# Two weight splits of the next expert ahead of the second half of SwiGLU

## The chip, the cores and the metric

One Trainium2 chip, one core. The time is device microseconds of one execution. The kernel before takes 1336.07 us, the median of three runs.

## The reference

One step of a one-layer streaming encoder over 576 tokens (512 of a prompt, 64 of a running stream): a projection, a pooling mixer beside gated linear attention, a layer norm, and then a mixture of 32 experts of which each token takes four. The change lies in the experts:

```python
def block_fn(args):
    e, rows = args
    xb = x2[rows]
    gu = jnp.dot(xb, w_gu[e]) + b_gu[e]
    gate, up = gu[:, :EXPERT_FF], gu[:, EXPERT_FF:]
    gate = jnp.minimum(gate, SWIGLU_LIMIT)
    up = jnp.clip(up, -SWIGLU_LIMIT, SWIGLU_LIMIT)
    hmid = gate * jax.nn.sigmoid(SWIGLU_ALPHA * gate) * (up + 1.0)
    return jnp.dot(hmid, w_down[e]) + b_down[e]
```

Everything is fp32. `w_gu` is 1024 x 2048 and `w_down` 1024 x 1024 for each expert, 12 MB an expert and 403 MB in all.

## The kernel before

Four engines and the queue of the sync engine run programs of their own and meet at semaphores. The first 290 us or so hold everything up to the router. Then a loop over 32 experts `n` runs on each engine, unrolled in Python. An expert's tokens, up to 96, are gathered from memory by GpSimd (`gather`), transposed by TensorE (`rows`), multiplied and scattered back (`scatter`).

**Weights.** The sync engine loads each expert in six pieces of 2 MB (`load`, line 448) into a ring of eight slots, `ring`. Pieces 0 to 3 are `w_gu`, 4 and 5 are `w_down`. Each load waits until its slot is free: for piece 1 of expert e that is the end of the `down` of expert e-2 (`down_read`), for the others a count of finished low splits (`split_done`).

**Splits.** Matmuls in fp16 need the weights as a high and a low fp16 half. Each piece is two pairs; an expert has ten pairs `p` that are split (the last piece is used in fp32 as it is). For each, ScalarE writes the high half (`hi`, line 802, called through `next_hi(n, p)`) and VectorE the low half (`lo`, line 1618, `next_lo(n, p)`), into four rotating buffers. So `hi` waits for the piece to have landed and for TensorE to have used the pair four before (`unit_used`), and `lo` waits for `hi`.

**One expert on TensorE.** Sixteen `unit`s (line 1173), two to a pair: the first half of gate (pairs 0 and 1, into `bank[2]`), the first half of up (2 and 3, `bank[3]`), then the second half of gate (4 and 5) and of up (6 and 7), both into `wide[0]`. Then the transposes of the next expert's rows, and `down` (line 1194) into `wide[1]`: first the fp16 part with pairs 8 and 9, then a part of 16 fp32 matmuls which reads `hm[:, 4:8]` and `w_down` from the ring, and which waits here:

```python
if k % 4 == 0:
    pe.wait_ge(hm_done, n * 2 + (k // 4 + 3))
```

**One expert on ScalarE.** `hi` of pairs 4 and 5, `gate(n, 0)`, pairs 6 and 7, `up(n, 0)`, pair 8, `hidden_hi`, pair 9, `gate(n, 1)`, `up(n, 1)`, then for the next expert pair 0, `rows_hi`, and pairs 1 to 3, then `weigh`, the output's evacuation. `gate` (line 816) is four evacuations (line 812) and a sigmoid (line 821), `up` (line 823) four evacuations and a clip (line 828).

**One expert on VectorE.** The low splits in the same order; `gated_half` (line 1593) multiplies gate and sigmoid, and `hidden` (line 1595, its instruction on line 1602) multiplies in up and signals `hm_done`. Behind `hidden(n, 1)` stand the low split of pair 0 of the next expert, `rows_lo`, `places_of`, and pairs 1 to 3.

Each engine carries out its program in the written order, so the order of these calls is the schedule. After the experts, the rows of four partial results (`part_rows`) are loaded back and summed with the last two experts' outputs, which TensorE adds, and a layer norm ends the kernel.

Of the kernel before, what the change touches and what calls it, by code (L numbers as in the profile page):

```python
# [50 lines left out]
E = 32  # L51
# [20 lines left out]
def build(nc, x_prompt, x_sample, state_pool, state_gla, w_in, w_pool, pool_scale, w_gate_up,  # L72
# [3 lines left out]
    with ExitStack() as ctx:  # L76
# [304 lines left out]
        def piece_slot(n, i):  # L381
            return (n * PER + i) % RING
# [6 lines left out]
        def landed(n, i):  # L389

            return 16 * (EARLIER[piece_slot(n, i)] + (n * PER + i) // RING + 1)
# [9 lines left out]
        def pair_done(n, p):  # L401

            return pairs(n) + (p + 1 + BUFS)
# [4 lines left out]
        def down_done(n):  # L408

            return n + 3  # L410
# [241 lines left out]
        def _(act):  # L652
# [45 lines left out]
            for t in range(TILES):  # L698
                n = ROWS[t]
# [84 lines left out]
            for t in range(TILES):  # L784
                n = ROWS[t]
# [5 lines left out]
                n = ROWS[t]  # L791
# [3 lines left out]
            def rows_hi(m, q):  # L795

                for b in range(2):
                    act.wait_ge(gT_ready, m * 2 + (b + 1))
                    act.activation(xhi[q][:, 4 * b:4 * b + 4, :], bank[b][:, 0:4 * BLK]
                                   .rearrange("p (k s) -> p k s", k=4), ACT.Copy, scale=X_UP).then_inc(gT_hi, 1)  # L800

            def hi(n, p, s, got):

                if p % 2 == 0:
                    act.wait_ge(slot_in[s], got)
                act.wait_ge(unit_used, pair_done(n, p) - BUFS)
                act.activation(whi[buf(n, p)], packed(s, p), ACT.Copy, scale=W_UP).then_inc(hi_done, 1)  # L807

            def from_limit(dst, b, at):

                for c in range(4):
                    last = act.activation(dst[:, c, :], b[:, c * BLK:(c + 1) * BLK], ACT.Relu, scale=-DOWN * S_UP,  # L812
                                          bias=bguT[:, at[0], at[1] + c:at[1] + c + 1])
                return last

            def gate(n, half, e):
                act.wait_ge(unit_used, pair_done(n, 4 * half + 1))
                act.wait_ge(hm_done, n * 2 + (half + 2))
                from_limit(g1, bank[2] if half == 0 else wide[0][:, 0:512], (e, 4 * half)).then_inc(gate_free, 1)
                act.wait_ge(gate_free, n * 2 + (half + 3))  # L820
                act.activation(sg, g1, ACT.Sigmoid, scale=-SWISH / S_UP, bias=sig_bias).then_inc(sig_done, 1)  # L821

            def up(n, half, e):
                act.wait_ge(unit_used, pair_done(n, 4 * half + 3))
                act.wait_ge(hm_done, n * 2 + (half + 2))
                from_limit(u1, bank[3] if half == 0 else wide[0][:, 512:1024], (e, 8 + 4 * half)).then_inc(up_free, 1)
                act.wait_ge(up_free, n * 2 + (half + 3))
                act.activation(u1, u1, ACT.Relu, scale=-1.0, bias=up_bias).then_inc(up_clip, 1)  # L828

            def hidden_hi(n):  # L830
                act.wait_ge(hm_done, n * 2 + 3)
                act.wait_ge(unit_used, pair_done(n - 1, 9))
                act.activation(hh, hm[:, 0:4, :], ACT.Copy, scale=1.0 / S_UP).then_inc(hh_done, 1)

            def weigh(n, p):

                act.wait_ge(down_read, down_done(n))
                if not isinstance(n, int):
                    act.wait_ge(scattered, n * 16 - 32)
                elif n > 0:  # L840
                    act.wait_ge(scattered, n * 16)
                act.activation(orow, wide[1 if isinstance(n, int) else 0][0:BLK, :], ACT.Copy, scale=slots[p][:, 5:6])\  # L842
                   .then_inc(out_ready, 1)

            def next_hi(n, p):
                hi(n, p, piece_slot(n, p // 2), landed(n, p // 2))
# [5 lines left out]
            for n in range(E):  # L852
                next_hi(n, 4)
                next_hi(n, 5)
                gate(n, 0, n)
                next_hi(n, 6)
                next_hi(n, 7)
                up(n, 0, n)
                next_hi(n, 8)
                hidden_hi(n)  # L860
                next_hi(n, 9)
                gate(n, 1, n)
                up(n, 1, n)
                if n + 1 < E:
                    next_hi(n + 1, 0)
                    rows_hi(n + 1, (n + 1) % 2)
                    next_hi(n + 1, 1)
                    next_hi(n + 1, 2)
                    next_hi(n + 1, 3)
                if n == 4:  # L870
                    act.wait_ge(bd_in, 16)
                    act.activation(y30_hi[BLK:P, :], bd, ACT.Copy)
                    act.activation(y31_hi[BLK:P, :], bd, ACT.Copy).then_inc(bd_hi, 1)
                if n + 2 < E:
                    weigh(n, n % ROW_BUFS)
                elif n + 1 < E:
                    act.wait_ge(down_read, down_done(n))
                    act.activation(y30_hi[0:BLK, :], wide[1][0:BLK, :], ACT.Copy, scale=slots[n % ROW_BUFS][:, 5:6])\
                       .then_inc(y30_high, 1)
# [27 lines left out]
            for t in range(RUN):  # L907
                n = HOLD
# [399 lines left out]
        def _(dve):  # L1308
# [6 lines left out]
            for t in range(TILES):  # L1315
                n = ROWS[t]
# [179 lines left out]
            for t in range(TILES):  # L1496
                n = ROWS[t]
# [92 lines left out]
            def gated_half(n, half):  # L1590

                dve.wait_ge(sig_done, n * 2 + (half + 1))
                dve.scalar_tensor_tensor(g1, g1, -LIMIT * S_UP, sg, ALU.add, ALU.mult).then_inc(gated, 1)  # L1593

            def hidden(n, half):

                dve.wait_ge(gated, n * 2 + (half + 1))
                dve.wait_ge(up_clip, n * 2 + (half + 1))
                dve.wait_ge(down_read, n + 2)
                if half == 0 and isinstance(n, int) and n > 0:  # L1600
                    dve.wait_ge(hh_done, n)
                dve.scalar_tensor_tensor(hm[:, 4 * half:4 * half + 4, :], u1, (1.0 - LIMIT) * S_UP, g1, ALU.add, ALU.mult)\  # L1602
                   .then_inc(hm_done, 1)

            def hidden_lo(n):
                dve.wait_ge(hh_done, n + 1)
                dve.scalar_tensor_tensor(hl, hm[:, 0:4, :], 1.0 / S_UP, hh, ALU.mult, ALU.subtract).then_inc(hl_done, 1)  # L1607
# [10 lines left out]
            def lo(n, p, s):  # L1618

                dve.wait_ge(hi_done, pairs(n) + (p + 1))  # L1620
                dve.wait_ge(unit_used, pair_done(n, p) - BUFS)
                dve.scalar_tensor_tensor(wlo[buf(n, p)], packed(s, p), W_UP, whi[buf(n, p)],  # L1622
                                         ALU.mult, ALU.subtract).then_inc(split_done, 1)

            def next_lo(n, p):
                lo(n, p, piece_slot(n, p // 2))
# [16 lines left out]
            for n in range(E):  # L1643
                if n + 2 < E:
                    onehot(n + 2, n + 2)
                next_lo(n, 4)
                if n == E - 1:
                    dve.wait_ge(y30_high, 1)
                    dve.scalar_tensor_tensor(y30_lo[0:BLK, :], wide[1][0:BLK, :], slots[(E - 2) % ROW_BUFS][:, 5:6],
                                             y30_hi[0:BLK, :], ALU.mult, ALU.subtract).then_inc(out_ready, 1)  # L1650
                next_lo(n, 5)
                gated_half(n, 0)
                next_lo(n, 6)
                next_lo(n, 7)
                hidden(n, 0)
                if n + 2 < E:
                    rows_of(n + 2, (n + 2) % ROW_BUFS, n - 2 if n >= 2 else None)
                if n == 1:
                    counts()
                if n == 5:  # L1660
                    dve.wait_ge(bd_hi, 1)
                    dve.tensor_tensor(y30_lo[BLK:P, :], bd, y30_hi[BLK:P, :], ALU.subtract).then_inc(bd_split, 1)
                if n == 6:
                    dve.memset(gatesT, 0.0).then_inc(gatesT_zero, 1)
                next_lo(n, 8)
                hidden_lo(n)
                next_lo(n, 9)
                gated_half(n, 1)
                hidden(n, 1)
                if n + 1 < E:  # L1670
                    next_lo(n + 1, 0)
                    rows_lo(n + 1, (n + 1) % 2)
                    places_of(n + 1, (n + 1) % ROW_BUFS)
                    next_lo(n + 1, 1)
                    next_lo(n + 1, 2)
                    next_lo(n + 1, 3)
            dve.wait_ge(unit_used, pair_done(E - 1, 9))
# [118 lines left out]
```

## Time and profile before

| | |
|---|---|
| time, median of three runs (lowest, highest) | 1336.07 us (1336.06, 1338.35) |
| the profiled execution: its time, its span | 1336.07 us, 1334.3 us |
| TensorE busy | 1254.9 us, 94% |
| VectorE busy | 1042.6 us, 78% |
| ScalarE busy | 941.8 us, 71% |
| GpSimd busy | 167.6 us, 13% |
| mean DMA rate | 354 GB/s |
| mean granted clock of TensorE | 0.983 |

The shares are means over the whole span, with the 290 us before the experts and the last 40 us in them. In a row of the order in time, the first number is the start in us from the span's start, the second how long the row's instructions take together; then the engine, the line, the operation, what it writes and reads, how many instructions are merged (x), and in square brackets the idle time ahead and what ended it. PE is TensorE, ACT ScalarE, DVE VectorE, SPq the queue of the sync engine.

### The profile page before, as it was taken

The page shows a single profiled execution, that of the slowest core. Times are in us where ns is not written, and L with a number is a line of the kernel's source. Part 1 is how long each engine was busy: PE and PEld are TensorE (multiplying, and loading weights), DVE is VectorE, ACT ScalarE, POOL GpSimd, SP SyncE. Part 2 cuts the span into 40 slices and gives each one's busy share as a digit, 9 for nine tenths or more (in the row PEclk, how much of TensorE's full clock was granted, in tenths as well). Part 3 has the DMA queues.
Part 4 walks back from the last instruction along what each step waited for, and adds up shares of the span by engine and source line. Part 5 has one row for each costly group of instructions (what it writes and reads, how often), then busy time and mean ns, then how long its engine had stood idle before and what let it go on. Part 6 is the DMA issues. An engine that isn't in the chain of part 4 may idle for free.

```text
span 1334.3 us, 35273 instructions
## 1 busy us (share of the span) xinstructions
PE 1254.9 (94%) x15514; PEld 902.6 (68%) x15514; DVE 1042.6 (78%) x1205; ACT 941.8 (71%) x1230; POOL 167.6 (13%) x139
## 2 busy tenths in 40 slices
PE   6999989979999999999999999999999999999985
PEld 3446655457777777777777777777777777777742
DVE  4442345478888899989989888888888888888877
ACT  4541221038888988899889888888888888888931
POOL 1000821011100001110010000111101111111002
PEclk9999999979999999999999999999999999999988
DMA  9550046059999999999999999999999999999983
GB/s 319 206 212 1 7 180 273 31 210 404 414 410 424 425 425 426 424 425 425 425 425 426 424 426 425 425 426 424 425 425 424 426 425 422 425 424 424 413 373 96
DMA packets 51033, 472.66 MB, mean 354 GB/s; under 512 B 9566, under 2 KB 10357, under 8 KB 25661
## 3 DMA queue, kind: packets, MB, share of 16 engines
q1 hardware_dynamic: 38860, 436.22, 78.3%
q0 software_dynamic: 11360, 31.77, 6.3%
q8 instruction: 125, 2.05, 0.6%
q10 hardware_dynamic: 656, 2.36, 0.5%
q14 instruction: 32, 0.25, 0.0%
HBM read 450.63 MB, written 29.95 MB: 360 GB/s over the span
## 4 chain that ended last, share of the span: by engine, by line
PE 38%; DMA 26%; DVE 6%; ACT 5%; issue 4%; SPq 0%; DVEq 0%; ACTq 0%; POOLq 0%
PE wide L917 27%; DMA ring<-in_w_gu 18%; PE bank L917 10%; DMA ring<-in_w_down 5%; ACT work L807 3%; DVE work L1622 3%; DMA work<-part_rows 2%; ACT work L812 1%; PE bank L1166 1%; DVE ring L1749 0%; DVE ring L1747 0%; DMA work<-h_rows,work 0%; DVE ring L1736 0%; DVE work L1607 0%; ACT work L828 0%
## 5 line engine op out<-in xcount | busy, mean ns | idle before, releaser
L1622 DVE SCALAR_TENSOR_TENSOR work<-ring,work 128x2048 f16<-128x2048 f32 x320 | 721.4, 2287 | 109.7 <-ACT work L807 95.3
L807 ACT ACTIVATE work<-ring 128x2048 f16<-128x2048 f32 x320 | 599.4, 1902 | 90.5 <-DMA ring<-in_w_gu 65.1
L917 PE MATMUL wide<-work 128*128 128x96 f16 (+3 forms) x7048 | 485.7, 230 | 36.9 <-DVE work L1607 10.9
L917 PEld LDWEIGHTS wide<-work 128*128 128x128 f16 (+3 forms) x7048 | 374.9, 102 | 131.9 <-issue 46.7
L917 PE MATMUL wide<-ring,work 128*96 128x512 f32 (+4 forms) x888 | 345.8, 545 | 1.0 <-ACT work L744 1.0
L917 PEld LDWEIGHTS bank<-work 128*128 128x128 f16 (+2 forms) x6482 | 296.8, 100 | 36.0 <-issue 23.7
L917 PE MATMUL bank<-work 128*128 128x96 f16 (+3 forms) x6482 | 304.6, 208 | 8.3 <-ACT work L780 3.8
L917 PEld LDWEIGHTS wide<-ring,work 128*96 128x96 f32 (+4 forms) x888 | 133.5, 151 | 190.0 <-issue 161.1
L607 POOL DMA_INDIRECT work<-h_rows,work x32 | 62.0, 1939 | 466.6 <-PE bank L1166 445.0
L620 POOL DMA_INDIRECT part_rows<-work x30 | 43.6, 1454 | 379.6 <-ACT work L842 379.6
L812 ACT ACTIVATE work<-wide,work 128x96 f32<-128x96 f32 x256 | 64.9, 333 | 0.1
L812 ACT ACTIVATE work<-bank,work 128x96 f32<-128x96 f32 x256 | 64.8, 333 | 0.0
L842 ACT ACTIVATE work<-wide,work 96x1024 f32<-96x1024 f32 x30 | 33.1, 1102 | 35.0 <-PE wide L917 35.0
L821 ACT ACTIVATE work<-work 128x384 f32<-128x384 f32 x64 | 39.4, 616 | 2.1
L828 ACT ACTIVATE work<-work 128x384 f32<-128x384 f32 x64 | 39.4, 616 | 2.1
L1500 DVE SCALAR_TENSOR_TENSOR ring<-ring,wide 128x1024 f32<-128x1024 f32 (+1 forms) x5 | 6.1, 1220 | 43.0 <-PE wide L917 43.0
L780 ACT ACTIVATE work<-bank 128x512 f32<-128x512 f32 (+1 forms) x10 | 5.0, 552 | 49.0 <-PE bank L1094 49.0
L917 PE MATMUL wide<-work,ring 128*128 128x512 f16 (+2 forms) x296 | 37.6, 285 | 0.0
L1602 DVE SCALAR_TENSOR_TENSOR work<-work 128x384 f32<-128x384 f32 x64 | 35.6, 556 | 1.4 <-DVE work L1593 0.2
L1166 PE MATMUL bank<-work 128*128 128x128 f32 x256 | 34.3, 277 | 2.0 <-DMA work<-h_rows,work 1.9
L1593 DVE SCALAR_TENSOR_TENSOR work<-work 128x384 f32<-128x384 f32 x64 | 35.3, 552 | 0.0
L1329 DVE SCALAR_TENSOR_TENSOR ring<-ring 128x1024 f16<-128x1024 f32 x16 | 19.0, 1222 | 20.9 <-ACT ring L695 20.9
(197 smaller groups left out, 637.8 us busy)
## 6 DMA issues: line engine op xcount, KB each, us to landing
ring<-in_w_gu SPq DMA_DIRECT2D x128, 2048.0 KB, 28.9
ring<-in_w_down SPq DMA_DIRECT2D x64, 2048.0 KB, 33.6
part_rows<-work POOLq DMA_DIRECT2D x1, 10240.0 KB, 36.8
ring<-in_w_in SPq DMA_DIRECT2D x4, 2048.0 KB, 13.6
ring<-part_rows SPq DMA_DIRECT2D x3, 2560.0 KB, 27.5
ring<-in_w_out SPq DMA_DIRECT2D x2, 2048.0 KB, 9.3
h_rows<-work POOLq DMA_DIRECT2D x1, 2560.0 KB, 9.9
ring<-h_rows SPq DMA_DIRECT2D x1, 2560.0 KB, 24.8
```

Of the source, the lines that this page charges most:

```text
L607: pool.indirect_dma_start(xg, None, h_dram, bass.IndirectOffsetOnAxis(ap=tok_i[q], axis=0), bounds_check=PLACES - 1, oob_is_err=False)\
L620: pool.indirect_dma_start(part_dram, bass.IndirectOffsetOnAxis(ap=dst_i[p], axis=0), orow, None, bounds_check=TOPK * SPAN - 1, oob_is_err= ...
L807: act.activation(whi[buf(n, p)], packed(s, p), ACT.Copy, scale=W_UP).then_inc(hi_done, 1)
L812: last = act.activation(dst[:, c, :], b[:, c * BLK:(c + 1) * BLK], ACT.Relu, scale=-DOWN * S_UP, bias=bguT[:, at[0], at[1] + c:at[1] + c + 1])
L821: act.activation(sg, g1, ACT.Sigmoid, scale=-SWISH / S_UP, bias=sig_bias).then_inc(sig_done, 1)
L828: act.activation(u1, u1, ACT.Relu, scale=-1.0, bias=up_bias).then_inc(up_clip, 1)
L842: act.activation(orow, wide[1 if isinstance(n, int) else 0][0:BLK, :], ACT.Copy, scale=slots[p][:, 5:6])\
L917: return pe.matmul(out, w, x, start=start, stop=stop, skip_group_check=True)
L1166: last = pe.transpose(bank[b][:, k * BLK:k * BLK + P], xg[:, (4 * b + k) * P:(4 * b + k + 1) * P], used)
L1593: dve.scalar_tensor_tensor(g1, g1, -LIMIT * S_UP, sg, ALU.add, ALU.mult).then_inc(gated, 1)
L1602: dve.scalar_tensor_tensor(hm[:, 4 * half:4 * half + 4, :], u1, (1.0 - LIMIT) * S_UP, g1, ALU.add, ALU.mult)\
L1622: dve.scalar_tensor_tensor(wlo[buf(n, p)], packed(s, p), W_UP, whi[buf(n, p)], ALU.mult, ALU.subtract).then_inc(split_done, 1)
```

## The change

Both programs call the same functions as before. On ScalarE the high splits of pairs 0 and 1 of the next expert move from behind `up(n, 1)` to between `gate(n, 1)` and `up(n, 1)`. On VectorE the low splits of the same pairs move to between `gated_half(n, 1)` and `hidden(n, 1)`. Pair 1 also moves ahead of `rows_hi`, and of `rows_lo` and `places_of`. The last expert has no next one and keeps its order.

```diff
                 hidden_hi(n)
                 next_hi(n, 9)
                 gate(n, 1, n)
+                if n + 1 < E:
+                    next_hi(n + 1, 0)
+                    next_hi(n + 1, 1)
                 up(n, 1, n)
                 if n + 1 < E:
-                    next_hi(n + 1, 0)
                     rows_hi(n + 1, (n + 1) % 2)
-                    next_hi(n + 1, 1)
                     next_hi(n + 1, 2)
                     next_hi(n + 1, 3)
                 if n == 4:
@@
                 hidden_lo(n)
                 next_lo(n, 9)
                 gated_half(n, 1)
+                if n + 1 < E:
+                    next_lo(n + 1, 0)
+                    next_lo(n + 1, 1)
                 hidden(n, 1)
                 if n + 1 < E:
-                    next_lo(n + 1, 0)
                     rows_lo(n + 1, (n + 1) % 2)
                     places_of(n + 1, (n + 1) % ROW_BUFS)
-                    next_lo(n + 1, 1)
                     next_lo(n + 1, 2)
                     next_lo(n + 1, 3)
```

## Rows read from the trace of the kernel before

**Rows 1.** The page: DMA rate in 40 slices; a line of DMA issues.

```profile
GB/s 319 206 212 1 7 180 273 31 210 404 414 410 424 425 425 426 424 425 425 425 425 426 424 426 425 425 426 424 425 425 424 426 425 422 425 424 424 413 373 96
...
ring<-in_w_gu SPq DMA_DIRECT2D x128, 2048.0 KB, 28.9
```

**Rows 2.** Stretches: length; busy PE, PEld, DVE, ACT, POOL; clock; DMA share; GB/s.

```profile
617.00:648.00 31.00, 30.77 (x466) 24.09 (x464) 28.31 (x29) 27.62 (x36) 2.63 (x2) 1.00 1.01 426
989.00:1020.00 31.00, 28.50 (x408) 21.60 (x406) 25.44 (x28) 27.01 (x35) 3.49 (x2) 1.00 1.01 425
```

**Rows 3.** TensorE in order of time: first matmuls of five experts.

```profile
331.55 8.51 PE L917 MATMUL bank<-work 128*128 128x96 f16 x197
...
576.92 8.51 PE L917 MATMUL bank<-work 128*128 128x96 f16 x197
...
606.64 5.56 PE L917 MATMUL bank<-work 128*128 128x96 f16 x127
...
848.05 9.11 PE L917 MATMUL bank<-work 128*128 128x96 f16 x197
...
1257.01 8.32 PE L917 MATMUL bank<-work 128*128 128x96 f16 x192
```

**Rows 4.** ScalarE waiting for weights: in order of time, and in the sums.

```profile
842.47 1.91 ACT L807 ACTIVATE work<-ring 128x2048 f16<-128x2048 f32 x1 [4.05 <-DMA ring<-in_w_gu]
...
ACT work L807 <- DMA ring<-in_w_gu: 65.1, 47, 4.1
```

**Rows 5.** ScalarE and VectorE in order of time, expert 9.

```profile
593.77 1.01 ACT L812 ACTIVATE work<-wide,work 128x96 f32<-128x96 f32 x4
594.81 0.62 ACT L821 ACTIVATE work<-work 128x384 f32<-128x384 f32 x1
...
608.94 3.89 ACT L807 ACTIVATE work<-ring 128x2048 f16<-128x2048 f32 x2 [0.99 <-PE bank L917]
...
594.36 2.29 DVE L1622 SCALAR_TENSOR_TENSOR work<-ring,work 128x2048 f16<-128x2048 f32 x1
596.56 0.56 DVE L1593 SCALAR_TENSOR_TENSOR work<-work 128x384 f32<-128x384 f32 x1
597.15 0.56 DVE L1602 SCALAR_TENSOR_TENSOR work<-work 128x384 f32<-128x384 f32 x1
...
610.88 4.49 DVE L1622 SCALAR_TENSOR_TENSOR work<-ring,work 128x2048 f16<-128x2048 f32 x2 [0.92 <-ACT work L807]
```

**Rows 6.** TensorE in order of time, expert 9: second part of `down`.

```profile
599.78 7.03 PE L917 MATMUL wide<-ring,work 128*96 128x512 f32 x16
```

**Rows 7.** The end: one piece of the chain, then VectorE in order of time.

```profile
1278.67 27.62 DMA work<-part_rows
...
1293.67 1.28 DVE L1727 SCALAR_TENSOR_TENSOR work<-wide,work 96x1024 f16<-96x1024 f32 x1
1294.87 11.00 DVE L1722 TENSOR_TENSOR ring<-ring 116x5120 f32<-116x5120 f32 x2
1310.05 1.23 DVE L1736 SCALAR_TENSOR_TENSOR ring<-wide,ring 116x1024 f32<-116x1024 f32 x1 [4.18 <-PE wide L917]
```

**Rows 8.** TensorE after idle gaps, and the clock in stretches after them.

```profile
993.91 5.38 PE L917 MATMUL wide<-work 128*96 128x512 f16 x24 [1.95 <-DVE work L1607]
...
1295.00 4.52 PE L917 MATMUL wide<-work 96*116 96x512 f16 x10 [4.98 <-DVE work L1727]
1299.32 4.54 PE L917 MATMUL bank<-work 128*116 128x512 f16 x20
1306.34 15.71 PE L917 MATMUL wide<-work 116*116 116x512 f32 x44 [2.49 <-DMA work<-part_rows]
...
992.50:995.50 3.00, 1.59 (x8) 0.96 (x9) 3.00 (x3) 2.97 (x10) 1.43 (x1) 1.00 0.99 421
1295.00:1299.00 4.00, 4.00 (x10) 2.16 (x11) 4.00 (x1) 0.00 (x0) 0.00 (x0) 0.50 0.62 262
1306.40:1309.50 3.10, 3.10 (x4) 1.35 (x5) 0.00 (x0) 0.00 (x0) 0.00 (x0) 0.50 0.06 24
```


## The prediction

> **What bounds the kernel now.** I read the page first: its 40 slices, for where the span is spent and at which DMA rate. From about 300 us until 1270 us the weight stream moves 404 to 426 GB/s [rows 1], beside a TensorE that the same page shows at nine tenths or more. Such averages hide who waits for whom, so the second view was the table of stretches [rows 2]. At 617 to 648 us TensorE works 30.77 of 31.00 us; at 989 to 1020 us it works 28.50 of 31.00, at the same 425 GB/s and the same full clock (2.4 GHz). The first is a stretch in which TensorE sets the pace; in the second something else does.
>
> What that is stands in the third view, the order in time. The first matmul of expert n, line 917 into `bank` (I call it the start of n), is at 331.55 us for expert 1, 576.92 for expert 9, 606.64 for expert 10, 848.05 for expert 18 and 1257.01 for expert 31 [rows 3]. From 9 to 10 that is 29.72 us; from 18 to 31 it is (1257.01 - 848.05)/13 = 31.46 us. In the late part ScalarE's first split of the next expert's weights waits for its landing: 4.05 us at 842.47 us [rows 4], and such waits add up to 65.1 us over the run [rows 4]. So there are two regimes. Until about expert 17 compute is the faster consumer (29.7 us from 9 to 10, (576.92 - 331.55)/8 = 30.7 on average before) of a stream that needs some 31.5 us an expert, and eats up the lead of the ring of eight slots; from then on the stream sets 31.46 us. An edit in the compute loop costs nothing as long as one expert's chain stays under that. It decides the kernel once it is over that.
>
> **The change, part by part.** Nothing is added or removed. Two splits of 128x2048 for expert n+1 go ahead of work of expert n, on both engines. No DMA is issued by either. What matters is what stood behind each queue's head.
>
> The chain of expert 9, before: ScalarE evacuates the gate half at 593.77 and its sigmoid starts at 594.81 and takes 0.62, so it is over at 595.43; the up half follows at once. VectorE runs its last low split at 594.36 (2.29 us), then `gated_half` at 596.56, then `hidden` at 597.15 (0.56, over at 597.71) [rows 5]. TensorE's second part of `down`, 16 fp32 matmuls that read this `hidden`, starts at 599.78, right behind the fp16 part, with no idle time ahead [rows 6]. So the slack of `hidden` is 599.78 - 597.71 = 2.07 us. It is the only cover that the change has.
>
> After: ScalarE starts the high split of pair 0 where `up` starts now, 595.34 (in these rows an instruction starts 0.08 to 0.09 us before the one ahead of it ends, as 596.56 against 594.36 + 2.29). Their waits hold nothing up in this regime: pairs 6 and 7 have been used by then, and the weights have landed. One split is 1.91 us [rows 4], so the high halves are there at 597.25 and 599.1. `up` is as long as `gate`, whose four evacuations start 1.57 us before the slot at 595.34, and ends at 600.7. VectorE is later still: its low split of pair 0 needs the high half, so it begins at 597.25; two in a row take 4.49 [rows 5], hence 601.74; `hidden` starts 0.08 before that and ends at 601.66 + 0.56 = 602.22. Queued behind it on VectorE are the rows, places and pairs 2 and 3 of the next expert, which TensorE needs only 7 us later; they are not late. The fp32 part of `down` starts a little after its releaser. Behind a landing at 1278.67 + 27.62 = 1306.29 the first matmul came 0.05 us later [rows 7, 8]; here a weight load of fp32 comes between, and I take 0.25. So it starts at 602.47 in place of 599.78: TensorE stands idle for 2.7 us. The next expert starts 6.86 us after that part begins (606.64 - 599.78): 609.33.
>
> So one expert takes 609.33 - 576.92 = 32.4 us. Is that a step that repeats? ScalarE's chain from the start of an expert hangs on TensorE alone: it waits for the first pair to be used (the idle 0.99 us ahead of 608.94, 2.30 us after the start), and from there to the sigmoid its work is gapless, so that the sigmoid ends 595.43 - 576.92 = 18.5 us after the start. A later start moves the whole chain, and nothing is won back by waiting. 32.4 is above the 31.46 that the stream takes, so the stream's waits disappear, and the sum goes by this chain in all experts, not only in the first half. Ring slots are released up to 2.7 us later within an expert, which a queue with a median of 28.9 us from issue to landing [rows 1] hides.
>
> The sum. Expert 1 starts at 331.55 + 2.69 = 334.2. Thirty experts at 32.41 are 972.3: expert 31 starts at 1306.5 (now 1257.0, so +49.5). Bounds: 32.3 (no latency ahead of the matmul, -4 in all) to 32.6 (extra Vector work in some experts, +5).
>
> The end, from the start of expert 31 to the end of the span: 1334.3 - 1257.0 = 77.3 us now. It is paced by a DMA queue that is still full: the last rows of `part_rows` are issued at 1278.67 and land 27.62 us later, and TensorE idles 2.49 us for them [rows 7, 8]. With the stream behind compute, that queue is empty and these loads land early. Then this chain remains: the second `down` part ends about 31 us after the start, the two halves of the last output are split off 2.4 later (1.28 for the low one [rows 7], about as much for the high one), and the two additions of 11.00 us together [rows 7] take VectorE to 44.5, where the first total starts at 53.0 now (1310.05 - 1257.01 [rows 7]). That gives back 8.5 us, the tail is 68.8. Span 1306.5 + 68.8 = 1375.3. The profiled execution took 1336.07 for a span of 1334.3, so 1.7 us lie outside; it is the median of the runs shown as well. **Time without any loss of clock: 1377 us.**
>
> **The clock.** The stall is new also in kind: 2.7 us without a matmul, once in each expert. The trace of before has few such gaps. After 1.95 us idle (at 993.91) the granted clock stayed at 1.00 in the rows around; after 4.98 us (at 1295.00) and after 2.49 us (at 1306.34) it was 0.50 [rows 8], that is 1.2 GHz. What it costs: ten 512-column matmuls take 4.52 us at half clock, twenty take 4.54 at full [rows 8], so work takes twice as long. The stretch at half clock after the gap of 2.49 us was at least 3.1 us [rows 8]; half of such a stretch is lost: 1.6 us, on the path, since it falls into the fp32 part of `down`. Bounds: no expert (as after 1.95) and all 31 (as after 2.49), 0 to 50 us. 2.7 is nearer to the gap that lost the clock, but experts that take more than 29.7 us now (30.7 on average before expert 9) have part of the gap already filled with a later fp16 part, so theirs is shorter. I take 18 of 31, 29 us: **1406 us**. The Trainium skill ("TensorE: Matmul & The Clock Gate", section "HAM oscillation — how this bites in real kernels") has an abstract rule that idle gaps up to a limit leave the clock alone, and that limit is longer than this stall; by it the sum would stay at 1377. The trace disagrees at 2.49 us, which is why I let the rows decide and keep the rule as a rival.
>
> **The rivals.** (a) The stall, but the clock stays: 1377 us. For it: the gap of 1.95 us, and long stretches with short gaps at clock 1.00 [rows 2]. Against: the gap of 2.49.
> (b) The change is hidden and the stream goes on setting the pace: 1336 us, same. It needs the chain to be at most 31.46 us, that is a stall of at most 1.7 us in place of 2.7. For it: the DMA rate, at its plateau of 425 GB/s in both stretches [rows 2]. Against: each term of the 2.7 is a row.
> (c) Faster: the first two splits free slots and fill buffers earlier, and the stream, which reached only 404, 414 and 410 GB/s in the slices 10 to 12 [rows 1], comes to 425. That is worth (21 + 11 + 15)/425 x 33.4 = 3.7 us: 1332. It decides only while `hidden` is less than 2.07 us later than now, since then nothing is lost on TensorE; I count 4.5 us later.
> (d) Worse than all the above: the clock falls in every expert and part of the releases comes too late as well: 1430 and more.
>
> **How the numbers follow.** Forecast (stall and clock losses in a good part of the experts) 0.60; (a) 0.25; (b) 0.07; (c) 0.03; (d) 0.05. The forecast's own range is 1385 to 1428. For 8 in 10, (a) must be inside with its bound of -4: 1373 to 1430. What a measurement of this kernel can tell from no change is about 0.2%, 2.7 us. Slower 0.90, same 0.07, faster 0.03.
>
> **What the profile of the changed kernel would show.** Right: idle time of 2 to 2.7 us ahead of the fp32 matmuls on `wide`, put down to the Vector line of `hidden`, in nearly every expert; starts 32.4 us apart where the clock holds and about 34 where it does not; the granted clock in the page below 9 tenths in many slices; ScalarE's waits for `in_w_gu` nearly gone; GB/s in the slices at 390 to 410 in place of 425; no wait for `part_rows` at the end. Wrong: if starts stay at 31.4 us and the waits for `in_w_gu` grow, then (b) holds and the step that failed is that ScalarE's chain is rigid. If starts are 32.4 apart throughout, the clock term is nought. What would upset all of it is a slot released too late for the stream: then a wait for `in_w_gu` would stand ahead of `up`.

## The result, and the profile after

The changed kernel takes 1386.01 us, the median of four executions (1383.43 to 1391.98), against 1336.07 before: slower, ratio 1.0378, 95% interval 1.0341 to 1.0413. The forecast was 1406 us, with 1377 us for the same chain without loss of clock. The profiled execution took 1395.49 us for a span of 1393.7.

First the page, in the lines that answer to [rows 1], with the shares of the chain that ended last, a line of the costliest groups and one of the DMA issues:

```profile
PEclk9999999889999999999999999999999999999998
...
GB/s 301 246 159 1 88 194 173 23 369 335 393 409 414 393 377 404 407 408 414 389 392 405 405 412 389 393 387 403 396 411 408 404 409 416 409 400 389 362 391 87
...
ACT 31%; PE 28%; issue 11%; DVE 9%; DMA 0%; POOL 0%; DVEq 0%; ACTq 0%; POOLq 0%
...
L918 PE MATMUL wide<-ring,work 128*96 128x512 f32 (+4 forms) x888 | 365.8, 570 | 54.6 <-DVE work L1603 53.6
...
ring<-in_w_gu SPq DMA_DIRECT2D x128, 2048.0 KB, 15.1
```

The two lines that answer to them on the page of before:

```profile
PE 38%; DMA 26%; DVE 6%; ACT 5%; issue 4%; SPq 0%; DVEq 0%; ACTq 0%; POOLq 0%
...
L917 PE MATMUL wide<-ring,work 128*96 128x512 f32 (+4 forms) x888 | 345.8, 545 | 1.0 <-ACT work L744 1.0
```

The stream no longer runs at its plateau of 425: from the 11th slice to the 37th it lies between 377 and 416 GB/s. Its pieces land 15.1 us after their issue and not 28.9, so the queue is about half as deep. ScalarE and TensorE share the chain that ended last, and DMA has 0% of it, where it had 26%. The fp32 matmuls on `wide` had 1.0 us of idle time ahead of them; now it is 54.6, of which 53.6 are put down to L1603, the instruction of `hidden` (lines after the edit are one higher than before). ScalarE no longer waits for `in_w_gu`, where [rows 4] had 65.1 us.

TensorE in order of time, experts 9 and 10, and two stretches of the table of stretches:

```profile
600.78 8.51 PE L918 MATMUL bank<-work 128*128 128x96 f16 x197
...
626.13 7.11 PE L918 MATMUL wide<-ring,work 128*96 128x512 f32 x16 [2.17 <-DVE work L1603]
633.08 3.10 PE L918 MATMUL bank<-work 128*128 128x96 f16 x69
...
658.44 8.80 PE L918 MATMUL wide<-ring,work 128*96 128x512 f32 x16 [2.08 <-DVE work L1603]
667.08 8.51 PE L918 MATMUL bank<-work 128*128 128x96 f16 x197
...
692.44 8.80 PE L918 MATMUL wide<-ring,work 128*96 128x512 f32 x16 [2.35 <-DVE work L1603]
```

```profile
626.00:633.00 7.00, 6.87 (x16) 2.62 (x17) 6.64 (x14) 2.80 (x2) 0.00 (x0) 1.00 1.03 438
658.50:662.10 3.60, 3.60 (x5) 1.31 (x6) 3.57 (x8) 2.60 (x2) 0.00 (x0) 0.54 1.01 424
```

Against [rows 3, 6]: expert 9 takes 633.08 - 600.78 = 32.30 us, where it took 29.72. Its fp32 part waits 2.17 us and then runs 7.11 us, at clock 1.00. In expert 10 the same part waits 2.08 us and takes 8.80 us: from 658.50 the clock is 0.54, and the expert takes 667.08 - 633.08 = 34.00 us. The next one, whose fp32 part is the row at 692.44, is of that kind too.

The two queues in order of time, expert 9, which answer to [rows 5]:

```profile
618.67 0.61 ACT L821 ACTIVATE work<-work 128x384 f32<-128x384 f32 x1
619.19 3.69 ACT L807 ACTIVATE work<-ring 128x2048 f16<-128x2048 f32 x2
622.79 1.01 ACT L812 ACTIVATE work<-wide,work 128x96 f32<-128x96 f32 x4
623.83 0.62 ACT L828 ACTIVATE work<-work 128x384 f32<-128x384 f32 x1
...
618.21 2.28 DVE L1623 SCALAR_TENSOR_TENSOR work<-ring,work 128x2048 f16<-128x2048 f32 x1
620.41 0.56 DVE L1594 SCALAR_TENSOR_TENSOR work<-work 128x384 f32<-128x384 f32 x1
621.11 4.49 DVE L1623 SCALAR_TENSOR_TENSOR work<-ring,work 128x2048 f16<-128x2048 f32 x2
625.52 0.55 DVE L1603 SCALAR_TENSOR_TENSOR work<-work 128x384 f32<-128x384 f32 x1
```

The sigmoid is over at 619.28, which is 18.50 us after the start, as before. Then ScalarE runs two splits for 3.69 us where `up` stood, and `up` ends at 624.45. VectorE starts its two low splits at 621.11, is through at 625.60, and `hidden` (L1603) ends at 626.07. The first fp32 matmul comes 0.06 us later.

`hidden` needs two things, and they arrive 1.15 us apart: `up` at 624.45 and the low splits at 625.60. The last to end is VectorE's, and that decides the 32.30. The chain that ended last has to be read with care here:

```profile
623.83 0.62 ACT work L828
...
624.49 1.12 DVE work L1623
625.61 0.48 DVE work L1603
```

It goes through `up` (L828) and shows only the last 1.12 us of the low splits, as if they had waited for `up`. The rows above show them at work without a pause from 621.11. What a chain through `up` alone gives is seen in experiment 1.

The end, which answers to [rows 7, 8]:

```profile
1325.04 8.32 PE L918 MATMUL bank<-work 128*128 128x96 f16 x192
...
1369.19 1.22 DVE L1738 SCALAR_TENSOR_TENSOR ring<-wide,ring 116x1024 f32<-116x1024 f32 x1
```

From the start of expert 31 to the first total it is 1369.19 - 1325.04 = 44.2 us (53.0 before), and nothing waits for `part_rows` any more.

### The profile page after: what moved, and what is told of

Its sections match the earlier page's. It is cut to its first block, busy times and chain, and to the rows that moved or that the text cites. A ratio compares the mean times of both kernels' runs of the same rounds, so it can differ in the third digit from the quotient of the medians.

```text
span 1393.7 us, 35273 instructions
## 1 busy us (share of the span) xinstructions
PE 1272.4 (91%) x15514; PEld 904.3 (65%) x15514; DVE 1040.4 (75%) x1205; ACT 939.4 (67%) x1230; POOL 143.5 (10%) x139
## 4 chain that ended last, share of the span: by engine, by line
ACT 31%; PE 28%; issue 11%; DVE 9%; DMA 0%; POOL 0%; DVEq 0%; ACTq 0%; POOLq 0%
ACT work L807 21%; PE wide L918 18%; PE bank L918 10%; ACT work L812 8%; DVE work L1623 4%; ACT work L828 2%; DVE work L1603 1%; DVE ring L1724 1%; ACT work L833 1%; DVE ring L1751 0%; DMA work<-h_rows,work 0%; DVE ring L1749 0%; DVE ring L1738 0%; DVE work L1532 0%; POOL work L647 0%
## 5 line engine op out<-in xcount | busy, mean ns | idle before, releaser
L918 PE MATMUL wide<-work 128*128 128x96 f16 (+3 forms) x7048 | 479.4, 229 | 23.1 <-issue 14.8
L918 PE MATMUL wide<-ring,work 128*96 128x512 f32 (+4 forms) x888 | 365.8, 570 | 54.6 <-DVE work L1603 53.6
L607 POOL DMA_INDIRECT work<-h_rows,work x32 | 52.7, 1647 | 505.5 <-PE bank L1167 481.3
L620 POOL DMA_INDIRECT part_rows<-work x30 | 27.9, 928 | 431.9 <-ACT work L842 431.9
L828 ACT ACTIVATE work<-work 128x384 f32<-128x384 f32 x64 | 39.4, 616 | 2.1
L1603 DVE SCALAR_TENSOR_TENSOR work<-work 128x384 f32<-128x384 f32 x64 | 35.4, 552 | 0.2 <-DVE work L1594 0.2
L1614 DVE SCALAR_TENSOR_TENSOR work<-bank,work 128x384 f16<-128x384 f32 x64 | 32.4, 548 | 3.3 <-ACT work L799 3.3
## 6 DMA issues: line engine op xcount, KB each, us to landing
ring<-in_w_gu SPq DMA_DIRECT2D x128, 2048.0 KB, 15.1
ring<-in_w_in SPq DMA_DIRECT2D x4, 2048.0 KB, 14.7
```

Of the source, the lines that this page charges most:

```text
L607: pool.indirect_dma_start(xg, None, h_dram, bass.IndirectOffsetOnAxis(ap=tok_i[q], axis=0), bounds_check=PLACES - 1, oob_is_err=False)\
L918: return pe.matmul(out, w, x, start=start, stop=stop, skip_group_check=True)
L1614: dve.scalar_tensor_tensor(xlo[q][:, 4 * b:4 * b + 4, :], bank[b][:, 0:4 * BLK] .rearrange("p (k s) -> p k s", k=4), X_UP, xhi[q][:, 4 * b ...
```

## The experiments

All of them ran next to the kernel before, on the same chip; ratios are against that. A line of three dots marks lines left out.

**1. ScalarE's half alone.** The first hunk of the change, not the second.

```diff
                 gate(n, 1, n)
+                if n + 1 < E:
+                    next_hi(n + 1, 0)
+                    next_hi(n + 1, 1)
                 up(n, 1, n)
                 if n + 1 < E:
-                    next_hi(n + 1, 0)
...
-                    next_hi(n + 1, 1)
```

> ScalarE's two splits ahead of up as in the change, VectorE's order as before. Theory (one expert's chain sets the pace): up ends 23.7 us after the start of an expert, hidden at 24.3, the fp32 part of down starts at 24.3 in place of 25.36, so an expert takes 31.2 to 31.3 us in place of 32.30, expert 31 starts near 1271, the tail gives back 8: 1342 us, and gaps of about 1.4 us cost no clock. Rival (VectorE's splits are harmless, ScalarE's do all the damage): 1377 us or more. Rival (the stream sets the pace as long as the chain is under 31.5): 1336 us.

Measured: 1345.75 us (1342.82 to 1346.58), ratio 1.0055 (1.0034 to 1.0076): 9 us slower, small but clear of noise. TensorE, ScalarE and VectorE in order of time, expert 9:

```profile
586.50 8.51 PE L918 MATMUL bank<-work 128*128 128x96 f16 x197
...
610.87 7.11 PE L918 MATMUL wide<-ring,work 128*96 128x512 f32 x16 [1.00 <-DVE work L1603]
617.82 2.37 PE L918 MATMUL bank<-work 128*128 128x96 f16 x52
...
609.55 0.61 ACT L828 ACTIVATE work<-work 128x384 f32<-128x384 f32 x1
...
610.26 0.56 DVE L1603 SCALAR_TENSOR_TENSOR work<-work 128x384 f32<-128x384 f32 x1 [3.57 <-issue]
```

617.82 - 586.50 = 31.32 us an expert, and this holds from expert 3 to 30 to within 0.01. `up` ends at 610.16 and `hidden` starts 0.10 us later, with VectorE idle before it: it now waits for `up`, not for a low split, and the idle time of TensorE is 1.00 us. The clock did not fall inside any expert. The theory was 4 us short, since it had 31.2 to 31.3 for the chain, which is 31.32, and expert 31 near 1271, which starts at 1275.52. The rival that ScalarE's part does all the damage is out by 30 us.

The other rival, that the stream sets the pace as long as the chain is under 31.5 us, is out as well, and that corrects the prediction. Here the chain is 31.32, nothing waits for `in_w_gu`, and the kernel is 9 us slower. The 31.46 us were the pace of the late experts alone. From expert 1 to 31 the kernel before took (1257.01 - 331.55)/30 = 30.85 us an expert [rows 3], because its first half went faster. A chain of 31.32 is above that average. Expert 1 starts 4.2 us later here (335.79), the thirty turns take 14.3 more, and the tail, 1344.8 - 1275.5 = 69.3 us in place of 77.3, gives back 8.0. Turned around, these terms say how long the chain may be in every turn before the span of 1334.3 is exceeded: (1334.3 - 335.8 - 69.3)/30 = 31.0 us, an estimate from this one execution.

**2. VectorE's half alone.** The second hunk, not the first.

```diff
                 gated_half(n, 1)
+                if n + 1 < E:
+                    next_lo(n + 1, 0)
+                    next_lo(n + 1, 1)
                 hidden(n, 1)
                 if n + 1 < E:
-                    next_lo(n + 1, 0)
...
-                    next_lo(n + 1, 1)
```

> VectorE's two splits ahead of hidden, ScalarE's order as before. Theory: VectorE's split of pair 1 now waits for ScalarE to come through up, the split of pair 0, rows_hi and the split of pair 1 (over at 24.5 us after the start), so hidden ends at 27.2 and an expert takes 34.2 us: 1434 us if the clock holds, 1485 if the longer gap of about 4.3 us costs the clock in every expert, which I expect. Rival (the cost is two splits of 2.3 us on VectorE however they are fed): about 1386 us, as the change.

Measured: 1483.48 us (1474.75 to 1490.69), ratio 1.1076 (1.1015 to 1.1138). TensorE in order of time for experts 10 and 12, VectorE in expert 10:

```profile
659.76 8.51 PE L917 MATMUL bank<-work 128*128 128x96 f16 x197
...
687.05 7.11 PE L917 MATMUL wide<-ring,work 128*96 128x512 f32 x16 [3.06 <-DVE work L1602]
694.00 6.20 PE L917 MATMUL bank<-work 128*128 128x96 f16 x142
...
758.31 10.15 PE L917 MATMUL wide<-ring,work 128*96 128x512 f32 x16 [3.32 <-DVE work L1602]
...
681.68 2.29 DVE L1622 SCALAR_TENSOR_TENSOR work<-ring,work 128x2048 f16<-128x2048 f32 x1 [1.72 <-ACT work L807]
684.24 2.29 DVE L1622 SCALAR_TENSOR_TENSOR work<-ring,work 128x2048 f16<-128x2048 f32 x1 [0.26 <-ACT work L807]
```

Expert 10 takes 694.00 - 659.76 = 34.24 us, as worked out (34.2). VectorE waits 1.72 us and 0.26 us for ScalarE's high splits ahead of `hidden`: it is held by the order of another engine's queue, not by its own work. In expert 12 the fp32 part takes 10.15 us, 3.0 more than with the clock up. So the time is right in part by luck: 5 of 31 experts keep the clock, which the forecast had falling in all, and in others a fall costs up to 3.0 us and not 1.7.

**3. One pair in place of two.** Only pair 0 ahead, on both engines.

```diff
+                    next_hi(n + 1, 0)
                 up(n, 1, n)
                 if n + 1 < E:
-                    next_hi(n + 1, 0)
                     rows_hi(n + 1, (n + 1) % 2)
...
+                    next_lo(n + 1, 0)
                 hidden(n, 1)
                 if n + 1 < E:
-                    next_lo(n + 1, 0)
                     rows_lo(n + 1, (n + 1) % 2)
```

> Only pair 0 moves ahead, on both engines. Theory: VectorE is through its split at 22.6 us after the start, hidden ends at 23.1 and the fp32 part starts at 23.15, 0.3 later than the fp16 part ends at best; 30.1 us an expert is under the stream's 31.46, so the time is that of before, 1336 us, with ScalarE's waits for the stream back. Rival (every split ahead costs its own length): 1377 less half of 41, 1356 us. Rival (an early split helps the stream): 1332 us.

Measured: 1337.77 us (1335.39 to 1340.33, ten executions), ratio 1.0003 (0.9988 to 1.0018): same. TensorE and ScalarE in order of time, and ScalarE's wait for the stream in the sums:

```profile
611.00 8.51 PE L918 MATMUL bank<-work 128*128 128x96 f16 x197
...
634.17 7.11 PE L918 MATMUL wide<-ring,work 128*96 128x512 f32 x16
641.12 1.06 PE L918 MATMUL bank<-work 128*128 128x96 f16 x21
...
844.66 1.91 ACT L807 ACTIVATE work<-ring 128x2048 f16<-128x2048 f32 x1 [2.50 <-DMA ring<-in_w_gu]
```

```profile
ACT work L807 <- DMA ring<-in_w_gu: 17.2, 14, 2.5
PE wide L918 <- DVE work L1603: 13.4, 12, 2.1
```

An expert of the first half takes 641.12 - 611.00 = 30.12 us, 0.4 more than before, and in the second half the wait for `in_w_gu` stands where the theory has it, now between the sigmoid and `up`. It adds up to 17.2 us where it was 65.1; what it delays shows as idle time of TensorE ahead of the fp32 part, 13.4 us. A chain that is longer than before, but shorter than the 30.85 us that an expert took on average, costs nothing here.

**4 and 9. Work in the gap.** The changed kernel with six matmuls in an unused part of `bank[2]` ahead of the fp32 part; nobody reads them.

```diff
                 first = 4 if isinstance(n, int) else 0
+                if isinstance(n, int) and n + 1 < E:
+                    for _ in range(6):
+                        mm(bank[2][:, 384:512], ident, ident, True, True)
                 for k in range(first, KT):
```

> The change, with six fp32 matmuls of 128x128 ahead of the fp32 part of down, results unused, about 0.7 us of TensorE work in a gap of 0.5 to 2.35 us. Theory (the clock falls in some experts for lack of work, 1.7 us each time): fewer falls or none, starts 32.3 us apart, 1377 us and a smaller spread between runs. Rival (the 34.0 us experts have another cause, the clock only coincides): 1386 us and the same spread as the change.

> The change with six 128x128 fp32 matmuls of TensorE in the gap. Theory: no fall of the clock inside the experts, 3 to 6 us under the unaltered change on the same chip, spread about half. Rival: no difference from the unaltered change.

Measured: 1381.46 us in experiment 4 (ratio 1.0331, 1.0309 to 1.0353). In experiment 9 it ran beside the unaltered change (experiment 8): 1380.75 us (1378.38 to 1382.80, ratio 1.0329, 1.0304 to 1.0354) against 1391.23 (1381.81 to 1396.52). TensorE in order of time, expert 12:

```profile
720.15 1.50 PE L918 MATMUL bank<-work 128*128 128x128 f32 x12
722.67 7.11 PE L918 MATMUL wide<-ring,work 128*96 128x512 f32 x16 [1.01 <-DVE work L1606]
```

The idle time left is at most 1.02 us, and in the two profiled executions no expert has a long fp32 part. So the clock theory holds, though 1381.46 lies between its 1377 and the rival's 1386. The six matmuls appear as twelve instructions and take 1.50 us, twice what I had reckoned, so that in some experts they end after `hidden` and cost a little themselves. The trace of experiment 9 says how much: its thirty turns from expert 1 (333.90) to expert 31 (1308.54) take 2.4 us more than the changed kernel's would without a fall (972.2, worked out below), and its tail is 1.0 longer, which stays unexplained. With these two, 1376.8 comes to 1380.2; this execution took 1379.89. Two forecasts of experiment 9 were too small: it is 10.5 us under the unaltered change, not 3 to 6, and its executions spread over 4.4 us against 14.7, less than the half expected.

**5. Three pairs.** One more pair ahead, on both engines.

```diff
                     next_hi(n + 1, 0)
                     next_hi(n + 1, 1)
+                    next_hi(n + 1, 2)
                 up(n, 1, n)
...
                     next_lo(n + 1, 0)
                     next_lo(n + 1, 1)
+                    next_lo(n + 1, 2)
                 hidden(n, 1)
```

> Pairs 0, 1 and 2 of the next expert ahead, on both engines. Theory: one more low split of 2.24 us ahead of hidden, so the fp32 part starts at 27.6 us after the start and an expert takes 34.5 us: 1446 us if the clock holds; gaps of 3 to 4.6 us cost it in every expert, 1.7 us each: 1497 us. Rival (the clock term is nought): 1446 us.

Measured: 1526.42 us (1523.30 to 1529.95), ratio 1.1422 (1.1384 to 1.1460). TensorE in order of time for experts 8 and 17, and stretches around the start of their fp32 parts:

```profile
597.14 8.51 PE L918 MATMUL bank<-work 128*128 128x96 f16 x197
...
624.72 7.11 PE L918 MATMUL wide<-ring,work 128*96 128x512 f32 x16 [3.40 <-DVE work L1603]
631.66 8.51 PE L918 MATMUL bank<-work 128*128 128x96 f16 x197
...
930.66 8.51 PE L918 MATMUL bank<-work 128*128 128x96 f16 x197
...
958.24 10.13 PE L918 MATMUL wide<-ring,work 128*96 128x512 f32 x16 [4.29 <-DVE work L1603]
968.21 0.97 PE L918 MATMUL bank<-work 128*128 128x96 f16 x19
```

```profile
618.00:624.50 6.50, 3.32 (x16) 1.62 (x14) 6.50 (x4) 6.47 (x10) 0.23 (x1) 1.00 1.00 423
957.00:963.50 6.50, 5.26 (x7) 1.84 (x8) 5.55 (x14) 1.71 (x1) 0.00 (x0) 0.54 1.01 427
```

Expert 8 kept its clock (1.00) through a gap of 3.40 us and takes 631.66 - 597.14 = 34.52 us, as worked out. Expert 17 takes 968.21 - 930.66 = 37.55: the clock is 0.54 over 6.5 us, and the fp32 part takes 10.13 us. Two of the 31 experts, 7 and 8, keep the clock. The theory holds in the chain and in the direction of the clock term, and was 29 us short in its size, since a fall is longer here.

**6 and 7. A lighter stream.** From expert 2 on, half of piece 3 is not loaded, and the bytes that the slot held are used in its place; in the kernel before (6) and in the changed one (7).

```diff
+                whole = src.rearrange("a p n -> (a p) n")
+                if isinstance(e, int) and e >= 2 and i == 3:
+                    sp.dma_start(ring[:, s * SLOT:s * SLOT + SLOT // 2], whole[:, 0:SLOT // 2])\
+                      .then_inc(slot_in[s], 16)
+                    return
...
```

> The kernel before; from expert 2 on half of piece 3 (1 MB of 12) is not loaded, the old bytes are used. Theory (late experts of the kernel before are paced by the stream): the stream needs some 2.4 us less an expert, the chain of about 30.1 us takes over, expert 31 starts near 1238: 1309 us. Rival (compute sets the pace in both): 1336 us.

> The changed kernel with the same half of piece 3 left out from expert 2 on. Theory (its pace is the chain through hidden, the stream is behind cover): as the change, 1386 us, 1377 to 1397 by the number of clock falls. Rival (releases that come late slow the stream and the stream still paces it): 30 x 2.4 us less, about 1315 us.

Measured: 1316.90 us (1313.78 to 1317.29), ratio 0.9848 (0.9818 to 0.9878), for 6; 1388.33 us (1383.56 to 1394.10), ratio 1.0386 (1.0340 to 1.0432), for 7. TensorE in order of time, first of 6 in the late part, then of 7:

```profile
1216.41 8.32 PE L922 MATMUL bank<-work 128*128 128x96 f16 x192
...
1246.11 2.08 PE L922 MATMUL bank<-work 128*128 128x96 f16 x45
...
1018.77 8.80 PE L923 MATMUL wide<-ring,work 128*96 128x512 f32 x16 [2.14 <-DVE work L1608]
```

With 8% less to load, the kernel before gains 20 us and its expert 30 takes 1246.11 - 1216.41 = 29.70 us, where the late experts took 31.46 on average [rows 3]. The changed kernel gains nothing. Both give wrong outputs, since old bytes are used; only the time is of interest. This is the plainest evidence for the two regimes: the one is paced by the stream late, the other never is. The gain is 8 us smaller than forecast: experts of 30 to 31 us are still frequent in 6, and the forecast had expert 31 near 1238, which starts at 1246.

**8. The change once more.** Unaltered.

> The changed kernel once more, unaltered, next to the filled one on one chip. Theory: experts of 32.30 us and experts of 34.0 us, the latter exactly those with a fall of the clock; a time of 1377 plus 1.7 us for each fall, 1383 to 1395 over the executions, with the mean granted clock falling as the time rises. Rival (the spread has another cause): no relation between clock and time.

Measured: 1391.23 us (1381.81 to 1396.52), ratio 1.0400 (1.0362 to 1.0437). Each execution's time and mean granted clock:

```
unaltered change (8)   1381.81 0.982   1386.46 0.980   1390.22 0.978   1392.23 0.975   1393.50 0.975   1396.52 0.973
gap filled (9)         1378.38 0.987   1378.48 0.985   1379.89 0.985   1381.61 0.984   1382.12 0.984   1382.80 0.984
```

Within each kernel the clock never rises with the time, over 15 us in the unaltered change, whose spread is a little wider at both ends than the 1383 to 1395 forecast. Not all of that spread need come from the gaps: the kernel before, whose profiled execution has no long fp32 part in any expert, spread from 1332.69 to 1340.45 us beside it, at clocks from 0.985 to 0.978.

**10. ScalarE's first pair alone.** The high split of pair 0 ahead of `up`, VectorE's order as before.

> ScalarE's high split of pair 0 alone ahead of up, VectorE's order as before. Theory: up ends at 21.9 us after the start in place of 20.1, hidden at 22.5, still before the fp16 part of down ends (22.85 at best), so nothing is late and the stream sets the pace: same as before, 1336 us. Rival (an early split helps the stream get to its plateau): 1332 us. Rival (any delay of up is paid in full): 30 x 1.8 us more less the stream's 1.1 an expert, about 1355 us.

Measured: 1336.78 us (1331.74 to 1340.72, twelve executions), ratio 0.9999 (0.9981 to 1.0016): same. A 1.8 us later `up` is covered, and no gain from the early split can be told from nothing. One thing here and in experiment 3 was not foreseen. Late in the loop, where the split waits for the stream ahead of `up`, TensorE idles and the clock can fall:

```profile
784.18 8.80 PE L918 MATMUL wide<-ring,work 128*96 128x512 f32 x16 [2.13 <-DVE work L1603]
```

Three experts of experiment 10 and one of experiment 3 have such a part of 8.80 us, and the times are those of before: where the stream is the bound, such a part costs nothing that the time shows.

## Why the prediction was right, point by point

**Two regimes.** Right that there are two, and shown by 6 and 7 together, and by 3 and 10, which lengthen the chain within the cover at no cost. Wrong in where the limit lies. The prediction has it that an edit "costs nothing as long as one expert's chain stays under" 31.46 us, and (b) is priced by it. In experiment 1 the chain is 31.32 and the kernel 9 us slower. The limit lies below that, by the estimate there at about 31.0: what counts is the average over the whole loop, 30.85, and what the tail gives back. The forecast is untouched by this, since its sum goes by the chain from expert 1 on, and 32.4 is above both.

**The slack of `hidden` and the stall.** Right in kind, and a little too large. The period is 32.30 us, forecast 32.41; the stall is 2.35 us at most, forecast 2.7. I had put 0.25 us between `hidden` and the first matmul, which is 0.06, and had measured the gap from the start of the next row, which lies before the end of the fp16 part. Which engine's splits matter is shown by 1: without VectorE's in front an expert takes 31.32 us, so of the 2.6 us that an expert gained, 1.0 is VectorE's order on top of ScalarE's.

**The chain is rigid.** Right. The sigmoid ends 18.5 us after the start in the changed kernel too, and the period repeats in experiment 1 and in the experts of the changed kernel that keep their clock.

**The sum.** For the profiled execution it closes: expert 1 starts at 335.9 (334.2 forecast, and 1.7 for a fall of the clock in expert 0), thirty periods of 32.30 are 969.0, some Vector work in experts 1, 5, 6 and 23 adds 3.2, and ten falls after expert 1 17.0; that makes 1325.1, measured 1325.04. The tail is 1393.7 - 1325.0 = 68.7 us, forecast 68.8. Without its eleven falls, at 1.70 each, the execution would have taken 1395.49 - 18.7 = 1376.8 us; forecast 1377. That this is so near is in part luck: thirty periods were put 3.3 us too high (32.41 for 32.30), and the 3.2 us of Vector work, which only the bounds had, made up for it.

**The clock.** The mechanism is right, one of its sizes is off. A fall costs 1.70 us (34.00 - 32.30), forecast 1.6. I assumed falls in 18 of 31 experts; there are 11 in the profiled execution and 8 in that of experiment 8, counted by the fp32 parts of 8.7 to 8.8 us in place of 7.1. The median of 1386.01 amounts to (1386.0 - 1376.8)/1.7 = 5.4, an estimate that puts all of the difference down to falls. So the step that was mis-sized is "I take 18 of 31", worth 20 us of the distance. Two of its reasons are shown. The gaps are 0.5 to 2.35 us and not 2.7: in the profiled execution 16 of 31 are 1.97 us or longer, in that of experiment 8 it is 13 at 1.88 or longer, and no shorter one was followed by a long fp32 part in either. And the length of a long gap does not settle the matter: 11 of those 16 and 8 of those 13 lost the clock, 2.35 us both lost and kept it, and with three pairs moved a gap of 3.40 us kept it. Which of the long gaps lose it stays open; it varies from execution to execution of one kernel. The rule of the Trainium skill ("TensorE: Matmul & The Clock Gate", section "HAM oscillation — how this bites in real kernels"), by which gaps under its limit are harmless, does not hold for the rows at 658.44 and 692.44, where gaps of 2.08 and 2.35 us are followed by half clock. Rival (a), 1377 us, was reached by no execution of the unaltered change; the fastest took 1381.81.

**What I expected of the profile.** Most of it came: idle time ahead of the fp32 matmuls in every expert up to 30, periods of 32.3 and 34.0, no waits for `in_w_gu` nor for `part_rows`, a stream under its plateau. But the idle time is between 2 and 2.7 us only in about half of the experts, 1.7 on average (53.6/31). And the page's clock line stays at nine tenths from the tenth slice to the last but one; a fall is too short against a slice of 35 us to be seen there, and the table of stretches has to be asked.

**The rivals.** (b) falls by the result, which is 50 us away, and by 1, 6 and 7. (c) is not borne out by 3 and 10. (d) did not happen here; experiment 5 shows what it looks like.

No version that loads all the bytes beats the kernel before. Those of 3 and 10 are equal to it. That the bytes set this limit is borne out by 6, where 8% fewer bytes made it 1.5% faster.

## What to carry to other kernels

In a loop that is paced by a stream, ask how long one turn of the compute chain may become before it is the bound. Start from the average over the whole loop, 30.85 us here, and not from the pace of the part in which the stream is waited for, 31.46: the fast first half (29.72 from expert 9 to 10) counts too. Ask also where in the chain the slack lies: here 2.07 us between `hidden` and its reader. Work for the next turn that is put ahead of the last link of this one is paid at the head of every queue that feeds the link, and the last of them to be through decides. To move it in one queue alone can be worse than in both, if that queue then waits for the other: 34.24 us with VectorE's half against 32.30 with both. A new idle gap of TensorE in each turn can cost more than its length, so look at the length of the matmuls behind it, not only at the gap.

## What was not expected of the hardware

Gaps of TensorE around 2 us were followed by half clock in some experts and not in others of the same execution, and one gap of 3.40 us was not. Behind gaps of 3.32 and 4.29 us (experiments 2 and 5, where every turn has a gap of 2.6 us or more and most have a fall) the fp32 part lost 3.0 us in place of 1.7. An fp32 matmul of 128x128 by 128x128 took 0.25 us (1.50 for six) and was recorded as two instructions.
